# Three-round projections for three mixers, and six weight pieces in another ring slot

## The reference, cut to what matters

```python
def mla_mix(x, w_in, q_norm_g, kv_norm_g, w_uq, w_ukv, pos):
    c_q, c_kv, k_r, q_mem = jnp.split(
        x @ w_in, [MLA_Q_RANK, MLA_Q_RANK + MLA_KV_RANK, MLA_Q_RANK + MLA_KV_RANK + MLA_ROPE], axis=-1)
...
def nsa_mix(x, w_in, kc, vc, ks, vs, kw_pad, vw_pad, slopes):
    q, gates, q_mem = jnp.split(x @ w_in, [TOK_WIDTH, TOK_WIDTH + TOK_HEADS * NSA_BRANCHES], axis=-1)
...
def rglru_mixer(h, w_in, conv_w, conv_b, w_a, b_a, w_x, b_x, lam, w_out):
    proj = h @ w_in
    xb, yb = jnp.split(proj, 2, axis=-1)
    y_gate = jax.nn.gelu(yb)
    xc = sum(xp[:, j:j + S] * conv_w[j] for j in range(CONV_W)) + conv_b
```

## Time and profile before

| what | value |
|---|---|
| median of three runs | 3039.74 us |
| the profiled execution | 3038.78 us |
| its span | 3037.1 us |
| PE busy | 2995.1 us (99%) |
| DVE busy | 2322.8 us (76%) |
| ACT busy | 1524.1 us (50%) |
| POOL busy | 106.0 us (3%) |
| stage of norm 0 (first product by tile to the end of piece 2) | 194.5 to 217.2 us |
| stage of norm 3 (to the end of piece 4) | 722.4 to 756.0 us |
| stage of norm 8 (to the end of piece 4) | 2088.7 to 2126.0 us |

### The profile page before, as it was taken

One profiled execution on the slowest core, in us unless ns is written; L12 is line 12 of the kernel. 1 busy time (PEld: TensorE's weight loads), 2 busy tenths in 40 slices (PEclk: granted clock), 3 DMA queues, 4 the chain that ended last, 5 costly groups with the idle time before them and its releaser, 6 DMA issues.

```text
span 3037.1 us, 52882 instructions
## 1 busy us (share of the span) xinstructions
PE 2995.1 (99%) x18680; PEld 2671.9 (88%) x18680; DVE 2322.8 (76%) x4347; ACT 1524.1 (50%) x2649; POOL 106.0 (3%) x130
## 2 busy tenths in 40 slices
PE   9999999999999999999999999999999999999998
PEld 7886887888688899899999988888799999988887
DVE  8866887886676789789899855555689889965555
ACT  5436543543554465555544455553755544445554
POOL 1010111101000000000000000000000000000000
PEclk9999999999999999999999999999999999999999
DMA  8763786876135542355544455555355544455554
GB/s 341 284 266 115 254 302 250 297 283 222 49 139 207 180 167 84 112 174 187 174 142 142 144 192 193 192 193 193 111 174 187 187 147 144 140 179 193 193 193 152
DMA packets 124977, 567.84 MB, mean 187 GB/s; under 512 B 13872, under 2 KB 14000, under 8 KB 97328
## 3 DMA queue, kind: packets, MB, share of 16 engines
q1 hardware_dynamic: 108864, 504.41, 48.1%
q0 software_dynamic: 15264, 58.73, 5.6%
q10 hardware_dynamic: 720, 3.00, 0.2%
HBM read 565.03 MB, written 1.05 MB: 186 GB/s over the span
## 4 chain that ended last, share of the span: by engine, by line
PE 88%; DVE 3%; ACT 2%; issue 0%; DMA 0%; DVEq 0%; SPq 0%; ACTq 0%
PE turn L365 47%; PE gather L365 40%; ACT arena L1508 1%; PE turn L986 0%; ACT hT L1508 0%; DVE arena L2472 0%; DVE arena L2467 0%; ACT L1508 0%; DVE arena L2520 0%; DVE keyed L2163 0%; DVE arena L2487 0%; ACT expert_src_high L1508 0%; DVE arena L2160 0%; ACT dense L1508 0%; DMA ring<-stream 0%
## 5 line engine op out<-in xcount | busy, mean ns | idle before, releaser
L1508 ACT ACTIVATE dense<-ring 128x1024 fp32r<-128x1024 f32 x542 | 573.8, 1059 | 372.8 <-PE gather L365 345.9
L2835 DVE TENSOR_TENSOR ring_low<-ring,dense 128x1024 fp32r<-128x1024 f32 x542 | 659.8, 1218 | 55.7 <-ACT dense L1508 52.8
L365 PE MATMUL turn<-expert_src_high,ring_low 128*128 128x256 f32 x2472 | 689.0, 279 | 0.0
L365 PE MATMUL turn<-expert_src_high,dense 128*128 128x256 f32 x2288 | 651.5, 285 | 0.2
L365 PE MATMUL turn<-expert_src_low,dense 128*128 128x256 f32 x2288 | 636.4, 279 | 0.0
L365 PE MATMUL gather<-dense 128*128 128x512 f32 x2048 | 630.8, 389 | 1.3 <-DVE dense L2970 1.3
L365 PE MATMUL turn<-rounded 128*128 128x512 f32 x1392 | 479.6, 390 | 0.3 <-ACT rounded L1508 0.3
L365 PEld LDWEIGHTS turn<-expert_src_high,ring_low 128*128 128x128 f32 x2472 | 464.7, 188 | 0.0
L365 PEld LDWEIGHTS gather<-dense 128*128 128x128 f32 x2048 | 384.4, 188 | 81.5 <-issue 1.7
L365 PEld LDWEIGHTS turn<-expert_src_high,dense 128*128 128x128 f32 x2288 | 430.6, 188 | 0.6 <-DVE ring_low L2835 0.6
L365 PEld LDWEIGHTS turn<-expert_src_low,dense 128*128 128x128 f32 x2288 | 429.7, 188 | 0.0
(11 more groups left out here) (270 smaller groups left out, 3916.5 us busy)
## 6 DMA issues: line engine op xcount, KB each, us to landing
ring<-tiles_in SPq DMA_DIRECT2D x544, 512.0 KB, 3.3
ring<-stream SPq DMA_DIRECT2D x205, 1024.0 KB, 5.5
arena<-ada_in POOLq DMA_DIRECT2D x96, 512.0 KB, 4.5
arena<-tables_in POOLq DMA_DIRECT2D x6, 1024.0 KB, 7.5
arena<-keys_in SPq DMA_DIRECT2D x2, 1024.0 KB, 7.3
arena<-c_in POOLq DMA_DIRECT2D x3, 512.0 KB, 6.0
hT<-x_in SPq DMA_DIRECT2D x1, 1024.0 KB, 5.0
x_rows<-rows_in ACTq DMA_DIRECT2D x1, 1024.0 KB, 21.7
```

The lines of the kernel that those rows point to most:

```text
L365: return nc.tensor.matmul(out, lhsT, rhs, start=start, stop=stop, skip_group_check=True)
L1508: return nc.scalar.activation(out, in_, func, **kw)
L2835: V.tensor_tensor(tile_words(t, ring_low).bitcast(R32), tile_words(t), tile_high[:, t % AHEAD, :], ALU.subtract).then_inc(S("tile_low"), 1)
```

## The change

16 of the 24 halves that `project_pair` or its like multiplied in these stages go the three-round way (`PARTED`): both halves of piece 2 and the second half of piece 1 of the latent projections, pieces 2 to 4 of the sparse attention's queries, and of the recurrent unit's inputs the second half of piece 1 and pieces 2 to 4. The first halves of pieces 1 (`project_half`) and the pieces multiplied by tile stay as they are.

- Norms 0, 3 and 8 get `source_high` on ACT and `parted_source` on DVE: 8 roundings and 8 subtractions each. POOL's conditions stay as they were.
- ACT (`parted_high`) copies 3, 4 and 3 halves straight after the norm; for the queries the last two after it has taken bank 0, for the recurrent unit two each after banks 0 and 1. DVE (`parted_low`) subtracts them at the answering places: behind the norm and ahead of `mla`, `adaptive` and `lru`, then in `nsa` behind two fills, and in `lru` ahead of the second and third convolution.
- The rounded copies go to parts of the arena that are free then (`PARTED_HOMES`, `PARTED_LOW`).
- `slot_of`: pieces 189 to 194 go one ring slot lower (piece 189 from slot 3 to slot 2). SP's single wait for all 272 tiles becomes one wait per piece: in the slots that hold tiles (0 to 2) for the last tile of that slot, in the others for all. For piece 189 this is tile 270 by count.
- The counts of `high_ready`, `low_ready`, `source_high` and `source_ready` are moved on accordingly (`part_base`, `source_base`).

The diff, cut to its core:

```diff
+        def slot_of(q):
+
+            first = PIECES_BEFORE[0]
+            return (q - (first <= q < first + SLOTS)) % SLOTS
+
+        def in_slot(q):
+            return [p for p in range(q) if slot_of(p) == slot_of(q)]
+
         def piece_there(q):
-            return piece_loaded[q % SLOTS], 16 * (q // SLOTS + 1)
+            return piece_loaded[slot_of(q)], 16 * (len(in_slot(q)) + 1)
...
+        PARTED = {
+            "mla": [(1, 1), (2, 0), (2, 1)],
+            "nsa": [(i, b) for i in range(2, 5) for b in range(2)],
+            "lru": [(1, 1)] + [(i, b) for i in range(2, 5) for b in range(2)]}
+        PARTED_BEFORE = {"mla": 1, "nsa": 3, "lru": 6}
+
         def part_base(stage):
 
-            return 2 * FFN_PIECES * stage - sum(s <= stage for s in WHOLE)
+            return 2 * FFN_PIECES * stage - sum(s <= stage for s in WHOLE) \
+                + sum(len(PARTED[p]) for p, s in PARTED_BEFORE.items() if s <= stage)
+
+        def parted_count(name, i, b):
+
+            stage = PARTED_BEFORE[name]
+            before = part_base(4) + 24 if name == "lru" else part_base(stage) + (stage in WHOLE) - len(PARTED[name])
+            return before + PARTED[name].index((i, b)) + 1
+
+        def source_base(stage):
+            return KC * (stage + sum(s <= stage for s in PARTED_BEFORE.values()))
+
+        def parted_source_base(name):
+            return source_base(PARTED_BEFORE[name]) - KC
...
-            sp.wait_ge(tile_done, LAYER_TILES)
             for q in range(*PIECES_BEFORE):
-                sp.wait_ge(piece_done, q - SLOTS + 1)
-                load(q, q % SLOTS)
+                last = in_slot(q)[-1]
+                if last >= PIECES_BEFORE[0]:
+                    sp.wait_ge(piece_done, last + 1)
+                elif slot_of(q) < TILE_SLOTS // 2:
+                    sp.wait_ge(tile_done, 1 + max(t for t in range(LAYER_TILES) if tile_home(t) == slot_of(q)))
+                else:
+                    sp.wait_ge(tile_done, LAYER_TILES)
+                load(q, slot_of(q))
...
+        PARTED_HOMES = {
+            "mla": homes("mla", aligned(qh_at), 2) + homes("mla_last", aligned(vh_at), 1),
+            "nsa": homes("nsa_first", aligned(phase), 3) + homes("nsa", aligned(biased_at) + KC * T, 2)
+            + homes("nsa_last", aligned(vh_at), 1),
+            "lru": homes("lru", lru_a_at, 7)}
+        PARTED_LOW = {"mla": over("mla_low", aligned(probs_at), KC, T),
+                      "nsa": over("nsa_low", aligned(biased_at), KC, T), "lru": over("lru_source_low", lru_h_at, KC, T)}
...
+            def project_half(bank, q, f):
+                w = slot(q, 2, KC, P)
+                for k in range(KC):
+                    last = mm(bank[:, f * T:(f + 1) * T], w[:, f, k, :], hT[:, k, :], k == 0, k == KC - 1)
+                return last
+
+            def parted_half(name, bank, q, i, b):
+                if (i, b) == PARTED[name][0]:
+                    pe.wait_ge(S("source_ready"), parted_source_base(name) + KC)
+                pe.wait_ge(S("low_ready"), parted_count(name, i, b))
+                home = PARTED_HOMES[name][PARTED[name].index((i, b))]
+                out = bank[:, b * T:(b + 1) * T]
+                for k in range(KC):
+                    wh = home[:, k * P:(k + 1) * P].bitcast(R32)
+                    wl = ring_low[:, slot_of(q), b * HALF + k * P:b * HALF + (k + 1) * P].bitcast(R32)
+                    xh, xl = expert_src_high[:, k, :].bitcast(R32), PARTED_LOW[name][:, k, :].bitcast(R32)
+                    mm(out, wh, xh, k == 0, False)
+                    mm(out, wh, xl, False, False)
+                    last = mm(out, wl, xh, False, k == KC - 1)
+                return last
+
             def mla_projections():
                 q0 = piece_base("mla_in")
                 for i in range(1, 3):
-                    arrive(pe, q0 + i)
-                    project_pair(q0 + i, B[i], hT).then_inc(piece_done, 1)
+                    if i == 1:
+                        arrive(pe, q0 + i)
+                        project_half(B[i], q0 + i, 0)
+                    else:
+                        parted_half("mla", B[i], q0 + i, i, 0)
+                    parted_half("mla", B[i], q0 + i, i, 1).then_inc(piece_done, 1)
...
-                    project_pair(q0 + 1 + i, B[i], hT).then_inc(piece_done, 1)
+                    for b in range(2):
+                        last = parted_half("nsa", B[i], q0 + 1 + i, 1 + i, b)
+                    last.then_inc(piece_done, 1)
...
             def lru():
                 q0 = piece_base("lru_in")
                 for i in range(1, 5):
-                    arrive(pe, q0 + i)
                     if i >= 4:
                         pe.wait_ge(S("lru_taken"), i - 3)
-                    project_pair(q0 + i, B[i % 4], hT).then_inc(piece_done, 1)
+                    if i == 1:
+                        arrive(pe, q0 + i)
+                        project_half(B[i], q0 + i, 0)
+                    else:
+                        parted_half("lru", B[i % 4], q0 + i, i, 0)
+                    parted_half("lru", B[i % 4], q0 + i, i, 1).then_inc(piece_done, 1)
...
+            def parted_high(name, halves):
+                for i, b in halves:
+                    q = piece_base(name + "_in") + i
+                    arrive(act, q)
+                    home = PARTED_HOMES[name][PARTED[name].index((i, b))]
+                    run(home[:, :].bitcast(R32), ring[:, slot_of(q), b * HALF:(b + 1) * HALF], ACT.Copy)\
+                        .then_inc(S("high_ready"), 1)
...
                     run(dst, B[i][:, :], ACT.Copy, scale=HD ** -0.5).then_inc(S("nsa_q_ready"), 1)
                     if i == 0:
+                        parted_high("nsa", PARTED["nsa"][4:])
                         act.wait_ge(S("gates_turned"), 1)
...
+                        if i < 2:
+                            parted_high("lru", PARTED["lru"][3 + 2 * i:5 + 2 * i])
...
-            layer_norm(0)
+            layer_norm(0, source_high(0, expert_src_high))
+            parted_high("mla", PARTED["mla"])
...
-            layer_norm(3)
+            layer_norm(3, source_high(3, expert_src_high))
+            parted_high("nsa", PARTED["nsa"][:4])
             nsa()
...
-            rms_norm(8)
+            rms_norm(8, source_high(8, expert_src_high))
+            parted_high("lru", PARTED["lru"][:3])
             lru()
...
+            def parted_source(name):
+
+                def chunk(k):
+                    dve.wait_ge(S("source_high"), parted_source_base(name) + k + 1)
+                    V.tensor_tensor(PARTED_LOW[name][:, k, :].bitcast(R32), hT[:, k, :], expert_src_high[:, k, :],
+                                    ALU.subtract).then_inc(S("source_ready"), 1)
+                return chunk
+
+            def parted_low(name, halves):
+                for i, b in halves:
+                    s, cols = slot_of(piece_base(name + "_in") + i), slice(b * HALF, (b + 1) * HALF)
+                    dve.wait_ge(S("high_ready"), parted_count(name, i, b))
+                    V.tensor_tensor(ring_low[:, s, cols].bitcast(R32), ring[:, s, cols],
+                                    PARTED_HOMES[name][PARTED[name].index((i, b))][:, :], ALU.subtract)\
+                        .then_inc(S("low_ready"), 1)
...
                 chain.add(V.memset(probs_c[:, :, :], 0.0))
+                parted_low("nsa", PARTED["nsa"][4:])
...
                 for pair in range(KC // 2):
+                    if pair in (1, 2):
+                        parted_low("lru", PARTED["lru"][1 + 2 * pair:3 + 2 * pair])
                     dve.wait_ge(S("lru_taken"), pair + 1)
...
-            layer_norm(0, ends(0))
+            layer_norm(0, ends(0), parted_source("mla"))
+            parted_low("mla", PARTED["mla"])
             mla()
...
-            layer_norm(3, ends(2))
+            layer_norm(3, ends(2), parted_source("nsa"))
+            parted_low("nsa", PARTED["nsa"][:4])
             adaptive()
             nsa()
...
-            rms_norm(8, 1, expert_ends(0))
+            rms_norm(8, 1, expert_ends(0), parted_source("lru"))
+            parted_low("lru", PARTED["lru"][:3])
             lru()
```

More of the change, by code:

```diff
@@ L679, in build, with homes @@
         gsum = pr.take(TT, 8)
+        def homes(name, at, n):
+            return [over(f"{name}_home{i}", at + i * HALF, HALF) for i in range(n)]
+        PARTED_HOMES = {
[5 more added lines that the diff above has]
+                      "nsa": over("nsa_low", aligned(biased_at), KC, T), "lru": over("lru_source_low", lru_h_at, KC, T)}
         @block.tensor
@@ L1601, in hin_half @@
                     act.wait_ge(*hin_used(h - 4))
[L1602 removed]
+                run(hin_high[h % 4][:, :].bitcast(R32), ring[:, slot_of(q), b * HALF:(b + 1) * HALF], ACT.Copy)\
                     .then_inc(S("high_ready"), 1)
```

49 lines of the change are left out of this document (27 added, 22 removed).

## The result

The changed kernel takes 3043.43 us (median of 20 runs, 3042.0 to 3046.17), the kernel before, on the same chip, 3038.66 us. The ratio is 1.0017, 95% interval 1.0011 to 1.0022: the change makes the kernel slower by 0.17%. That is a real difference in this many runs, and less than the 0.2% that the prediction named as its border, so it falls in the part that the prediction called "same" (0.35). The forecast was 3046.1 us, 6.4 us above the kernel before; measured are 4.8 us above it.

A forecast was written before the change was run, and what follows sets the result against it. PE bounds the kernel, 88% of the chain. Latent projections +6.0, queries +7.9, recurrent unit -7.5: +6.4 us on 3038.78, 3045.2; the median 1.0 higher, 3046.1 us. Range 3042.5 to 3050; for 8 in 10, 3037 to 3052.

The forecast's parts named there:

- same: Whole kernel: outcome within about 0.2%, 6.1 us, of the kernel before; chance 0.35.
- POOL into DVE's subtractions: Norms 0 and 3: POOL's x_rows update delays DVE's subtractions; PE stands 5.9 us in norm 0, 9.7 us in norm 3.
- The sum of 9.4 + 1.8 us: Norm 0: four POOL instructions, 9.4 us, plus five remaining DVE subtractions, 1.8 us, run from 200.5 to 211.7.
- the first rival: Norms 0 and 3: DVE keeps its turn, POOL holds it up once for 2.35 us; total 3028 us; chance 0.18.
- The queue ahead of `adaptive()`: Norm 3: four weight halves, 4 x 1.14 us, delay the gates' copy; without POOL still 1.1 us later.
- The saving of a half: All three stages: each converted half takes 2.80 instead of 3.46 us, saving 0.66; 16 halves save 10.5 us.
- The clock: Behind PE's new waits in norms 0 and 3: granted clock falls near 0.50, costing 2.1 us each (1.4 to 2.9).
- The recurrent unit: Norm 8: earlier first piece without clock drop gives 2.9 us, seven halves 4.6; together -7.5 us.
- (3,0) and (4,0): Recurrent unit: first halves of pieces 3 and 4, ready at 2106.9 and 2112.3, wanted by PE at 2107.35 and 2112.95.
- The second rival: Recurrent part gives -4.6 us, not -7.5; with the clock's larger price twice, 3049 to 3051 us; chance 0.14.
- the shift in norm 3: Second attention's queries: ACT's copy of the gates, and PE with it, moves from 734.23 to 743.95, +9.7 us.

The follow-up runs named there:

- experiment 3: The changed kernel with each of POOL's four instructions of 1024 columns split into two of 512: 3041.02 us, ratio 1.0008 against the kernel before.
- experiment 1: The changed kernel with POOL's x_rows update after norms 0 and 3 waiting for that stage's weight-half subtractions on DVE: 3027.41 us, ratio 0.9959 against the kernel before.
- experiment 4: The changed kernel with POOL's update after the weight halves and the small DVE operation ahead of norm 3: 3028.17 us, ratio 0.9961 against the kernel before.
- experiment 5: The changed kernel with unread products, 11 and 20, filling PE's two waits in norms 0 and 3: 3039.16 us, ratio 1.0002 against the kernel before.
- Experiment 8: The kernel of experiment 1 with eight unread products in PE's old 3.7 us break in the second attention's units: 3025.24 us, ratio 0.9957 against the kernel before.
- 7: The kernel before with only the slot move and the waits per slot, no rounded halves: 3035.48 us, ratio 0.9988 against the kernel before.
- 2: The changed kernel with the small DVE operation that ACT's exponential waits for moved ahead of norm 3: 3038.80 us, ratio 0.9998 against the kernel before.
- 6: The changed kernel with only the recurrent unit's seven rounded halves and the slot move, none in the other two stages: 3031.74 us, ratio 0.9977 against the kernel before.

## Why the prediction was right, step by step

**POOL into DVE's subtractions (the main term): right, and slightly too large.** POOL began at 200.02 (said: 200.4, in a stage that is 0.33 us earlier here), and DVE's subtractions of up to 2.58 us are what the text asked to see. The sum of 9.4 + 1.8 us was too long: from POOL's start to the end of the source it is 10.5 us and not 11.2, since the subtractions lengthen POOL's instructions by 0.05 to 0.17 us each and not by their own 0.36. So PE stood for 5.3 us and not 5.9 in norm 0, and in norm 3 for 9.1 (0.6 of it old), +8.5 and not +9.7. The Trainium skill (SBUF — State Buffer, Who interferes with whom) says that whoever issues first has the shared pair for the whole instruction while the other blocks; each single row here agrees. It does not spell out who comes next when both have a queue, the point on which the first rival hung; here they take turns. After's four subtractions of 2.3 to 2.6 us already speak against the rival, and experiment 3 against POOL going first throughout. The order of issue fits this: POOL's second instruction started at 202.50 and DVE's next subtraction at 202.63, POOL's fourth at 207.49 and DVE's at 207.62, each while the other's was still at work. That the prediction's sum of the two came close is luck in part: it had POOL's work count in full, and five subtractions happened to meet four POOL instructions. The rival's total, 3028, was near what the kernel gives with POOL out of the way, 3027.4, but not by its parts: it had -2.0 for the latent projections, where the table of experiment 1 has -0.3, and -1.3 to -2.8 for the queries, where it has -3.9.

**The queue ahead of `adaptive()`: right.** Its releaser chain is the one in the timeline. Without POOL the gates come 1.0 us later than before (said 1.1, experiment 1); only 0.6 of this goes with the place of the small operation (experiment 4), the rest with ACT's copies.

**The saving of a half: mis-sized.** The forecast took 2.80 us for 24 rounded products from one record group of the chain. By the distance between banks they are 2.83 us in norm 3 and 2.88 us in norm 8, so a half saves 3.46 - 2.83 = 0.63 and 3.46 - 2.88 = 0.58 us and not 0.66: 9 x 0.63 + 7 x 0.58 = 9.7 us for 16 halves, and not 10.5. The distance between two like starts in a full row would have been the better measure than the length of one group.

**The clock: right by mechanism in after, off by 0.5 and 0.3.** 2.6 and 1.8 us against 2.1 twice (experiment 5). The errors cancel, and in the first attention they hide each other: the wait was 0.6 us too long and the clock 0.5 too short, which is why +6.2 lies so near the said +6.0. That a wait of this size must bring the low clock doesn't hold in general: behind 3.13 us it stayed at 1.00 (experiment 3).

**The recurrent unit: right.** -7.2 us in the table (-3.2 and -4.1, before rounding) against -7.5 (-2.9 and -4.6): the halves gave 0.5 us less, the start 0.3 more. The piece was issued 1.33 us before the last product's end (said 1.4), no clock drop, no wait in five pieces; (3,0) and (4,0) were there 0.8 and 1.3 us before PE wanted them (said 0.4 and 0.65). The second rival, that this part gives less, didn't come true.

**What the forecast left out.** It held the rest of the kernel fixed. But the break in the second attention's units, 2.9 us before, is 1.7 us in after, with the same 3.7 us wait ahead of it: 1.2 us that no step of the sum has. So: 6.2 (said 6.0) + 6.7 (said 7.9) - 1.2 (said nothing) - 7.2 (said -7.5) = +4.5, against the forecast's +6.4. The terms that failed are the shift in norm 3, 9.7 us where 8.5 was measured, and this one, 1.2 us each; the halves' smaller saving went the other way.

The median of the kernel before is 3038.66 in the runs beside after and 3039.74 in those shown ahead of the prediction, so 1.1 of the 2.7 us by which 3046.1 missed is the base, and 1.6 the sum.

**The range.** The prediction gives its bounds once as 3043.5 to 3050 and later as 3042.5 to 3050; the single bounds that it lists add up to 3043.6 to 3051.9 around 3046.1. The measured 3043.43 lies at the lower edge: 0.07 us below the first range, inside the second.

## What to carry to other kernels

By these rows, two-input work on DVE and POOL's work on SBUF should not be due at the same time when PE waits for the DVE side: count one POOL instruction for every DVE instruction that meets it, and put POOL's work behind DVE's last urgent one (16 us here, for three lines). When conversion work is added ahead of PE, look for what small operation now stands behind it in each queue; one of 0.15 us cost 4.3 us here while POOL was in the way. A wait of PE costs its length and the clock behind it, and both can be read from the windows; filling a wait with products that nobody reads gave 1.7 to 2.6 us each time (experiments 5 and 8).

## What the runs showed of the hardware that was not expected

**Turns, not priority.** Held-up subtractions took up to 2.58 us beside POOL instructions of 1024 columns and up to 1.50 us beside such of 512 (experiment 3).

**A copy of DVE is held up as well.** In experiment 1 POOL's work was moved beside DVE's copies for the key. Before, the copy of 3072 elements on 32 partitions took 1.75 us; there it took 3.83, and POOL's last instruction, which met it, 3.74:

```profile
212.15 1.75 DVE L2396 COPY arena<-arena 32x3072 f32<-32x3072 f32 x1
```

```profile
212.16 3.83 DVE L2509 COPY arena<-arena 32x3072 f32<-32x3072 f32 x1
214.46 3.74 POOL L3192 TENSOR_TENSOR x_rows<-x_rows,arena 128x1024 f32<-128x1024 f32 x1
```

Nothing that PE needed waited for it. The Trainium skill names copies among the DVE instructions that can take the shared pair (SBUF — State Buffer, Who interferes with whom); these rows agree.

**The same break lowers the clock in one kernel and not in the next.** Kernels 1 and 8 have the same instructions up to norm 3. In the first attention PE waits twice for 1.19 us in both, with 1.05 us of work between, and the same twelve records follow, of kernel 1 and of kernel 8:

```profile
248.03 4.37 PE L369 MATMUL turn<-arena,ring 128*64 128x256 f32 x12 [1.19 <-DVE arena L2527]
```

```profile
248.11 2.77 PE L369 MATMUL turn<-arena,ring 128*64 128x256 f32 x12 [1.19 <-DVE arena L2530]
```

1.6 us hang on that, in one execution each. In before, after and kernels 3 and 7 the clock stayed up there, in kernels 2, 4, 5 and 6 it fell. Nor does the length of a wait decide: behind the 3.13 us of experiment 3 the clock stayed at 1.00, while in the kernel before it fell behind 2.66 us at norm 8. What decides was not settled. For a forecast it means that a sum over this kernel is not known to better than some 1.5 us, however well the stages are costed, and that differences of single executions of that size are no evidence. Experiment 8's second gain, and in part experiment 4's missing one, are of this kind.
